# Four products, then four subtractions, on GpSimd at the end of HGRN, and their copies between the evictions of the window's keys and values

## The reference

```python
for l in range(DEPTH_2):                       # 2
    h = _rmsnorm(x, g_mix[l])
    (a_cq, a_ckv, a_kr, b_q, b_ff, b_fb, b_i, b_g,
     c_q, c_k, c_v, gate_a, gate_b, gate_c) = _split_cols(h @ w_in[l], IN_SPLITS)
    y_a = _mla(a_cq, a_ckv, a_kr, ...)
    y_b = _hgrn2(b_q, b_ff, b_fb, b_i, b_g, ...)
    y_c = _window_gqa(c_q, c_k, c_v, rel_bias, c_sink[l])
    merged = (sigmoid(gate_a) * (y_a @ w_br_a[l]) + sigmoid(gate_b) * (y_b @ w_br_b[l])
              + sigmoid(gate_c) * (y_c @ w_br_c[l]))
    x = x + merged @ w_out[l]
    x = x + _cross(_rmsnorm(x, g_x[l]), ...)
    x = x + _swiglu(_rmsnorm(x, g_ffn[l]), ...)
```

```python
o = _rmsnorm(o_f + o_b, g_out) * jax.nn.silu(heads(g, B_DV))                       # y_b
s = einsum('bnqkgd,bnskd->bnkgqs', q, kb) * (C_DH ** -0.5) + bias                   # window
p = exp(s - m);  p = p / (sum(p) + exp(sink - m));  o = einsum(..., p, vb)
```

## Time and profile before

| | before |
|---|---|
| median of 3 runs | 4115.5 us (4111.91 to 4115.66) |
| the profiled execution | 4119.53 us |
| its span, from the first to the last instruction | 4117.7 us |
| TensorE busy | 3797.1 us, 92% of the span |
| VectorE, ScalarE, GpSimd busy | 47%, 35%, 20% |
| mean granted TensorE clock | 0.952 |

### The profile page before, as it was taken

The page is one execution under the profiler, slowest core; times in us unless marked ns, Lnnn a source line. Parts: engine busy times, 40 slices in busy tenths (PEclk is TensorE's granted clock), DMA queues, the critical chain, the costliest instruction groups (busy, mean ns, idle before and its releaser), DMA issues.

```text
span 4117.7 us, 59944 instructions
## 1 busy us (share of the span) xinstructions
PE 3797.1 (92%) x25270; PEld 3078.3 (75%) x25270; DVE 1945.4 (47%) x3078; ACT 1429.2 (35%) x2317; POOL 834.5 (20%) x838
## 2 busy tenths in 40 slices
PE   6888997989999989997999999998999799999998
PEld 3567886887888757786887778875677688777887
DVE  4555554544534464654334443346466523344333
ACT  3431122113323345744223332224565422243222
POOL 0123312321202022432111010102244211001010
PEclk8998998989999999998999999999999999999999
DMA  4321010002222201110222222221111022222222
GB/s 176 123 88 17 3 42 22 3 22 103 94 96 97 77 26 62 62 62 21 97 98 96 93 82 97 98 87 36 51 62 62 21 92 97 87 103 82 97 97 87
DMA packets 81106, 300.84 MB, mean 73 GB/s; under 512 B 8776, under 2 KB 9928, under 8 KB 79944
## 3 DMA queue, kind: packets, MB, share of 16 engines
q1 hardware_dynamic: 80840, 297.02, 21.0%
HBM read 292.79 MB, written 4.19 MB: 72 GB/s over the span
## 4 chain that ended last, share of the span: by engine, by line
PE 64%; DVE 9%; ACT 5%; issue 3%; POOL 2%; DVEq 0%; POOLq 0%; ACTq 0%
PE ps L205 63%; DVE he L244 1%; PE ps L210 1%; DVE wlo L236 1%; DVE hc L2333 1%; ACT ha L224 1%; ACT wp L225 1%; DVE ha L236 1%; DVE tmp L244 1%; DVE q L236 1%; ACT whi L224 0%; ACT L224 0%; DVE ws L244 0%; POOL u L236 0%; DVE hl L236 0%
## 5 line engine op out<-in xcount | busy, mean ns | idle before, releaser
L236 DVE TENSOR_TENSOR wlo<-wraw,whi 128x1024 fp32r<-128x1024 f32 x537 | 682.1, 1274 | 772.3 <-ACT whi L224 771.3
L205 PE MATMUL ps<-hh,whi 128*128 128x512 f32 x1840 | 733.1, 398 | 19.7 <-DVE hl L236 13.9
L205 PE MATMUL ps<-hl,whi 128*128 128x512 f32 x1840 | 723.8, 393 | 0.0
L205 PE MATMUL ps<-hh,wlo 128*128 128x512 f32 x1840 | 723.6, 393 | 0.0
L224 ACT ACTIVATE whi<-wraw 128x1024 fp32r<-128x1024 f32 x537 | 559.8, 1050 | 229.0 <-PE ps L205 171.6
L205 PEld LDWEIGHTS ps<-hh,whi 128*128 128x128 f32 x1840 | 350.0, 190 | 105.1 <-ACT hh L224 20.6
L205 PEld LDWEIGHTS ps<-hh,wlo 128*128 128x128 f32 x1840 | 349.9, 190 | 74.5
L205 PEld LDWEIGHTS ps<-hl,whi 128*128 128x128 f32 x1840 | 350.7, 191 | 70.4
L205 PE MATMUL ps<-u,u 64*64 64x64 f32 (+2 forms) x6016 | 241.2, 236 | 62.5 <-DVE u L236 47.6
L205 PEld LDWEIGHTS ps<-u,u 64*64 64x64 f32 (+1 forms) x6016 | 220.8, 146 | 81.8 <-DVE u L236 33.2
L236 POOL TENSOR_TENSOR gl<-fv,gh 128x512 fp32r<-128x512 f32 x66 | 85.4, 1294 | 593.7 <-ACT gh L224 593.7
(11 more groups left out here) (391 smaller groups left out, 7099.9 us busy)
## 6 DMA issues: line engine op xcount, KB each, us to landing
wraw<-weights SPq DMA_DIRECT2D x537, 512.0 KB, 3.2
x<-xT SPq DMA_DIRECT2D x2, 2048.0 KB, 11.9
bias_lines<-ln SPq DMA_DIRECT2D x1, 2048.0 KB
xmf<-memT SPq DMA_DIRECT2D x2, 1024.0 KB, 5.1
out<-x SPq DMA_DIRECT2D x1, 2048.0 KB, 6.2
bias<-bias_lines SPq DMA_DIRECT2D x1, 1536.0 KB, 8.5
con<-consts SPq DMA_DIRECT2D x1, 1378.0 KB, 9.6
ctxt<-ctxT SPq DMA_DIRECT2D x1, 1024.0 KB, 11.6
```

The lines of the kernel that those rows point to most:

```text
L205: self.last, self.open = self.e.matmul(out, lhsT, rhs, start=start, stop=stop, skip_group_check=skip), True
L236: return self.e.tensor_tensor(out, a, b, op)
```

## The change

`pool_hgrn_out` gets two loops in place of one: GpSimd first takes the four products, then the four subtractions. `act_window` calls `act_hgrn_out` (four copies) behind the eviction of the keys and the feed of one weight block, ahead of the eviction of the values, which stood in front of them. Both happen once in each of the two layers.

```diff
@@ pool_hgrn_out
             pool.wait_ge(dve.at("hn", l, i), dve.at("hgate", l, i))
             pool.tt(s3, L.G4[:, i, :], s2, ALU.mult).then_inc(pool("hy", l, i), 1)
             pool.also(f"ht2{l}", l, i)
+        for i in range(4):
+            s3 = L.t3[l, i]
             pool.wait_ge(K.act.at("hyh", l, i), pool.at("hy", l, i))
             pool.tt(K.Y["b"][1][:, i, :], s3, K.Y["b"][0][:, i, :].bitcast(F32), ALU.subtract).then_inc(pool("hyl", l, i), 1)
             pool.also(f"ht3{l}", l, i)
@@ act_window
         K.act_feed("wv", l)
+        K.act_hgrn_out(l)
         act.wait_ge(pe.at("wv", l))
         act.cp(L.wV.rearrange("p a b -> p (a b)"), ps["wv", l]).then_inc(act("wv", l), 1)
         act.also("ps", "wv", l)
-        K.act_hgrn_out(l)
         for i in range(9):
```

## The result

In the first measurement the changed kernel took 4083.44 us (median of 4 runs, 4078.81 to 4093.3) where the kernel before took 4113.7 (4109.17 to 4115.66 in 4 runs): ratio 0.9927, 95% interval 0.9909 to 0.9945, 30 us. In two further series it took 4094.07 (9 runs; before 4111.35 in 32 runs; ratio 0.9955, 0.9939 to 0.9970) and 4093.51 (5 runs; before 4119.22 in 9; ratio 0.9946, 0.9932 to 0.9959). The forecast was 4093.1 in a range of 4086 to 4100. The kernel is faster, and by how much is the question: 30 us, or about 20.

A forecast was written before the change was run, and what follows sets the result against it. TensorE was taken as bound, except for a 16.03 us gap per layer while VectorE waited for GpSimd's `ybl`. Gain 2 x 11.2 = 22.4 us, so 4115.5 - 22.4 = 4093.1 us, range 4086 to 4100.

The forecast's parts named there:

- What bounds the kernel: TensorE idles 16.03 us per layer after heads 0 and 1's scores; VectorE's additions wait for GpSimd's `ybl`, 3.22 us a tile.
- Products, copies, subtractions: HGRN output, layer 0: products end by 1853.1 to 1854.3, copies near 1859.1, subtractions by 1862.5 to 1863.2, all hidden.
- the port: GpSimd and VectorE's `wlo` contend for SBUF at two new meetings; up to 1.22 us lost at each, all hidden.
- The additions: VectorE's first additions wait for TensorE's scores; head 0's first maximum comes 2.83 us after them, 11.2 us earlier per layer.
- The clock term: TensorE's burst after the 4.9 us gap: clock still falls, so 0 gained, bounds 0 and 0.9 us per layer.
- All later stages follow the chain: After the window stage nothing is tied to wall time, so the full 11.2 us per layer reaches the end.
- The sum of 22.4: Total gain over both layers: 2 x 11.2 us, with nothing taken for the clock.
- The range: Whole kernel's time: 4086 to 4100 us, from the forecast's bounds and the earlier runs' 3.75 us spread on both sides.
- the clock stays high: Rival at TensorE's shortened gap: clock does not fall, 0.9 us more gained per layer, 4091.3 us; chance 0.08.
- ScalarE's move has no effect: Rival: copies still start only with the values' eviction; GpSimd's batching alone gains 6.0 us per layer, 4103.5 us; chance 0.06.
- The gain is given back: Rival: a wait behind the window stage stays where it was in time, no change, 4115.5 us; chance 0.05.
- The low clock: Rival: TensorE's low clock outlasts the gap, each head costs 4.6 us more over 7 heads, 4157 us; chance 0.02.

The follow-up runs named there:

- the parts alone: Two runs against the changed kernel: products in a row, copies left behind the values' eviction, 4101.38 us; copies ahead, each tile's product and subtraction kept together, 4095.33 us.
- the run with the gap filled: Changed kernel plus 16 further 128x512 matmuls on TensorE between the scores of heads 0 and 1 and the first transposes; 4086.86 us, one execution.

## Why the forecast came out as it did

- **What bounds the kernel**: right. The gap of some 16 us in each layer, the wait for GpSimd's `ybl`, and the four tiles going round at 3.22 us are what the parts alone take away.
- **Products, copies, subtractions**: right in place and size but for the port. The products took 6.04 us, where four alone at 1.22 us' spacing make 4.93; the subtractions 5.60, and 4.94 in the run in which no `wlo` stood beside them. Each `wlo` kept its 1.22 us. So GpSimd lost 1.1 and 0.7 us, under the 1.22 that I allowed for each, and all of it was hidden. One operation bore nearly all of it each time. The third product began 0.05 us behind a `wlo`, the first subtraction 0.50 us behind one:

```profile
1828.91 2.31 POOL L236 TENSOR_TENSOR ht<-hgt,ht 128x512 f32<-128x512 f32 x1
1835.79 1.88 POOL L236 TENSOR_TENSOR ybl<-ht,ybh 128x512 fp32r<-128x512 f32 x1 [3.31 <-ACT ybh L224]
```

The Trainium skill (SBUF — State Buffer, section Who interferes with whom) has it that of a VectorE and a GpSimd instruction that contend, issue order decides which one blocks. These two meetings agree: the `wlo` had begun first and kept its time, and GpSimd lost 1.0 and 0.6 us of the 1.17 and 0.73 us in which they overlapped.
- **The additions**: right. First maximum 2.83 us after the scores began, as forecast, 11.2 us saved at that point; gap 4.84 us for 4.9. The values were evicted 0.11 us after the scores' start in both kernels. One reading behind it was off: head 2's additions, the model for the 2.83, began when VectorE's own division of head 1 ended (1891.93 + 1.01 = 1892.94), not 0.93 us behind the scores because of TensorE. The 2.83 us still carried over, since in both cases the four additions were stretched by waiting for the scores (1.99 and 2.07 us, for 1.68 where the scores lay ready):

```profile
1891.93 1.01 DVE L240 TENSOR_SCALAR wp<-wp,sml 128x256 f32<-128x256 f32 x2
```

- **The clock term**: I took 0. It fell, as taken, but in the changed kernel the burst behind the gap became 0.4 us longer, because 6.15 us of it ran at 0.50 and not 5.24, a loss that my bounds of 0 and 0.9 excluded. The bound above was too low as well: at the full clock the burst was 2.1 us shorter, and VectorE's chain 1.3 us ahead. The wrong step was that GpSimd's division of head 1 holds the end of the burst. In the kernel before, that division and TensorE's own scores of head 2 happened to end together (1894.29 and 1894.36); in the run with the gap filled TensorE went on to head 1's transposes 1.4 us before the division ended.
- **"All later stages follow the chain"**: this step failed in its size. The sum of 22.4 became 18.3 us in the profiles, 10.1 of it between the two evictions of the values and 8.2 behind the second. Counted from layer 0's eviction of the keys, the changed kernel was 11.2 us ahead at head 0's first maximum and 10.7 at head 3's additions. At the window's last `ycl` it was 12.4 ahead of one profile of before and 10.5 ahead of the other, and behind the stretch shown above 10.3 and 8.6. So 0.4 to 0.5 us are lost in the burst of each layer and 2.0 in that one stretch, all at a lower mean clock. The rest of the 4.1 is what remains of gains and losses of up to 2 us, of which some lie between the two profiles of before themselves. I didn't trace it.
- **The range**: this is where the forecast of the time failed: 4083.44 us lies 2.6 us below it. The step was "the runs before differ by 3.75 us among themselves, which goes on both sides". Three runs understate it: 32 runs of the same kernel span 27 us. The first measurement had 4 runs of each kernel, and the profiled one of the changed kernel had a first stretch of 1844.3 us where the other profiles had 1855 or more. So 18 to 22 of its 30 us are the change's. The rest is the lot of those runs; of the other three no profile exists, and why the first stretch varies stays open. In the two later measurements the medians are 4094.07 and 4093.51, for a forecast of 4093.1. That they meet it within 1 us is partly luck: the gain was 4.1 us smaller than forecast, and the median of before came out 4.2 us lower in 32 runs (4111.35) than in the three that I had started from (4115.5).
- **The rivals**: "the clock stays high" didn't occur. "ScalarE's move has no effect" is excluded by the run without it, in which the additions came 5.6 us later than in the changed kernel (10.7 us gained for 18.5). "The gain is given back" has a fifth of truth: some 4 us, and what is traced of it goes with TensorE's lower clock, not with a weight load that stayed where it was in time. The low clock was gone within one burst, as before.

## What to carry to other kernels

When an engine's program alternates between two stages of a chain tile by tile, and the partner's copies stand behind a wait for a third engine, do all of the first stage, then all of the second, and put the partner's copies ahead of its long wait: each alone brought half or more, both together ended at the next floor. The next floor is readable beforehand, as the distance between the same two instructions where the same engine paces them (2.83 us here). And read a change of half a percent from a marker just ahead of it to the end, not from the whole span: that distance repeated within 0.4 us for the changed kernel and within 2 for the kernel before, where the totals of one kernel spread by 27. A range built on three runs says nothing of such a spread.

## What the runs showed of the hardware

- The time of the same 15063 matmuls in the first stretch differed by 19 us between executions of one program (1844.3, 1859.9, 1863.6), and the mean granted clock with it (0.958, 0.954 and 0.954 over the whole span).
- A gap of 4.84 us on TensorE was enough for the clock to fall to 0.50, 4.2 us into it. The burst behind it then ran at 0.66 on average, 6.15 us of it at 0.50, for 5.24 us behind a gap of 16.03; with 3.85 us of matmuls in the same gap the clock stayed at 1.00 and the burst took 7.03 us instead of 9.15.
- Delaying a stage by 1.5 us cost nothing in the end, in one execution: a later stretch at a mean clock of 0.95 became one at 0.96 and 2.1 us shorter.
- A GpSimd operation of 1.28 us took 2.31 us when a two-input VectorE operation of 1.22 us had begun 0.05 us ahead of it; the VectorE operation kept its time.
